# Attention pairs: a pair's factors and division one unit of scores later, and the latent key copies ahead of the last query tile's rotation

## What is computed

```python
s = jnp.einsum('bqkgd,btkd->bkgqt', qblk, k).astype(jnp.float32) * scale
p = jax.nn.softmax(s, axis=-1).astype(v.dtype)
return jnp.einsum('bkgqt,btkd->bqkgd', p, v)
...
merged = jnp.concatenate([rms_norm(o_g, out_norm_gqa), rms_norm(o_m, out_norm_mla)], axis=-1)
return merged @ w_o
```

## Time and profile before

| what | us |
|---|---|
| runs of the kernel, median (lowest to highest) | 2344.77 (2344.0 to 2347.44) |
| the profiled execution | 2343.82 |
| its span | 2341.9 |
| TensorE busy, share of the span | 2279.8 (97%) |
| TensorE's weight loads | 1636.5 (70%) |
| VectorE | 1332.9 (57%) |
| ScalarE | 879.0 (38%) |
| GpSimd | 230.0 (10%) |

### The profile page before, as it was taken

How to read it: one execution, slowest core, us unless ns; L and a number is a source line. 1 busy time by engine, 2 the same in 40 slices (tenths; PEclk the granted TensorE clock), 3 DMA queues, 4 the chain that set the end, 5 groups by cost and what they waited for, 6 DMA issues and landing times.

```text
span 2341.9 us, 28359 instructions
## 1 busy us (share of the span) xinstructions
PE 2279.8 (97%) x10908; PEld 1636.5 (70%) x10908; DVE 1332.9 (57%) x2055; ACT 879.0 (38%) x1518; POOL 230.0 (10%) x190
## 2 busy tenths in 40 slices
PE   7999999999998999999999999999999999999998
PEld 6755876444675588644457788888888778888886
DVE  5676654323657665433347757777435665877722
ACT  4475542111437644211133234444223233444421
POOL 2212201000220220100000011000001002000000
PEclk9999999999999999999999999999999999999999
DMA  4300439999530024899974333333333323333331
GB/s 174 99 5 24 141 149 386 409 410 410 210 99 15 19 90 180 339 408 410 410 299 122 86 90 90 99 98 92 99 98 136 112 77 91 99 99 98 101 97 48
DMA packets 112085, 381.62 MB, mean 163 GB/s; under 512 B 16464, under 2 KB 17232, under 8 KB 111696
## 3 DMA queue, kind: packets, MB, share of 16 engines
q1 hardware_dynamic: 108208, 366.80, 44.8%
q0 software_dynamic: 2304, 8.39, 0.9%
q10 hardware_dynamic: 1440, 4.62, 0.5%
HBM read 363.51 MB, written 6.29 MB: 158 GB/s over the span
## 4 chain that ended last, share of the span: by engine, by line
PE 87%; DVE 6%; ACT 3%; DMA 2%; POOL 1%; issue 1%; SPq 0%; POOLq 0%; DVEq 0%; ACTq 0%
PE ps L1349 11%; PE ps L1350 11%; PE ps L1351 11%; PE ps L1654 9%; PE ps L1373 5%; PE ps L1374 5%; PE ps L1375 5%; PE ps L1676 5%; PE ps L1535 3%; PE ps L1394 3%; PE ps L1392 3%; PE ps L1393 3%; PE ps L1485 2%; PE ps L1493 2%; PE ps L1686 1%; PE ps L1687 1%
## 5 line engine op out<-in xcount | busy, mean ns | idle before, releaser
L2464 DVE TENSOR_TENSOR wlo<-stage,whi 128x1024 fp32r<-128x1024 f32 x262 | 329.2, 1260 | 279.2 <-ACT whi L1793 278.6
L1349 PE MATMUL ps<-hTh,whi 128*128 128x512 f32 x1120 | 443.2, 396 | 0.0
L1351 PE MATMUL ps<-hTh,wlo 128*128 128x512 f32 x1120 | 438.0, 391 | 0.0
L1350 PE MATMUL ps<-hTl,whi 128*128 128x512 f32 x1120 | 437.7, 391 | 0.0
L1793 ACT ACTIVATE whi<-stage 128x1024 fp32r<-128x1024 f32 x262 | 276.0, 1057 | 328.4 <-PE ps L1375 120.7
L1349 PEld LDWEIGHTS ps<-hTh,whi 128*128 128x128 f32 x1120 | 211.6, 189 | 48.6 <-issue 4.7
L1351 PEld LDWEIGHTS ps<-hTh,wlo 128*128 128x128 f32 x1120 | 211.2, 189 | 44.7
L1350 PEld LDWEIGHTS ps<-hTl,whi 128*128 128x128 f32 x1120 | 211.6, 189 | 42.7
L2379 DVE TENSOR_TENSOR ps<-ps,Rs 128x512 f32<-128x512 f32 x124 | 86.0, 698 | 140.3 <-PE ps L1351 126.2
L2382 DVE SCALAR_TENSOR_TENSOR t<-ps,vecs,t 128x511 f32<-128x511 f32 (+1 forms) x176 | 131.0, 744 | 3.8 <-ACT t L1756 0.7
L2379 DVE TENSOR_TENSOR x<-x,ps 128x512 f32<-128x512 f32 x184 | 116.4, 680 | 28.5 <-PE ps L1375 18.0
(11 more groups left out here) (382 smaller groups left out, 4209.4 us busy)
## 6 DMA issues: line engine op xcount, KB each, us to landing
stage<-in_wpk SPq DMA_DIRECT2D x268, 512.0 KB, 3.6
wa<-in_wd SPq DMA_DIRECT2D x56, 512.0 KB, 15.5
wa<-in_wu SPq DMA_DIRECT2D x54, 512.0 KB, 15.1
wa<-in_wg SPq DMA_DIRECT2D x46, 512.0 KB, 14.3
ws<-in_wg SPq DMA_DIRECT2D x26, 512.0 KB, 12.4
ws<-in_wu SPq DMA_DIRECT2D x24, 512.0 KB, 11.1
wr<-in_wg SPq DMA_DIRECT2D x24, 512.0 KB, 15.2
stage<-in_wd SPq DMA_DIRECT2D x22, 512.0 KB, 16.4
```

The source lines that it names most:

```text
L1349: pe.matmul(o, h, ah, start=k == 0, stop=False)
L1350: pe.matmul(o, h, al, start=False, stop=False)
L1351: t = pe.matmul(o, lo, ah, start=False, stop=k == 7)
L2464: ve.tensor_tensor(M.wlo[i % NW][:, :], M.stage[i % NSTAGE][:, :], f(M.whi[i % NW][:, :]), ALU.subtract).then_inc(*S.wlo.mark(("w", i)))
```

## The change

It has two parts. First, the step `att_out` of the mixer is split. `att_copy` (ScalarE's copy of the values to `oT`) stays behind the values; the turn of the factors (`shares`), VectorE's product and all that `att_sums` puts off move into the next tick, which runs behind the next unit's scores. For the last pair (`p == 7`) they stay where they were. Second, the rotation of q3 is put off by two more ticks, so that in VectorE's program it comes behind the four copies of the latent keys.

```diff
@@ attention(), values()
             if kt == KT - 1:
-                b = self.take()
-                self.do("shares", l, p, b)
-                self.do("att_out", kind, l, p, ub[p], b)
+                self.do("att_copy", l, p, ub[p])
                 self.drop(ub[p])
-                self.drop(b)
-                self.att_sums(l, p)
+
+                def divide():
+                    b = self.take()
+                    self.do("shares", l, p, b)
+                    self.do("att_out", kind, l, p, b)
+                    self.drop(b)
+                    self.att_sums(l, p)
+                if p == 7:
+                    divide()
+                else:
+                    self.later.append(divide)
@@ mixer(), head_tile()
-                    self.later.append((lambda: self.last.append(st3)) if tile == "q3" else st3)
+                    if tile == "q3":
+                        self.last.append(lambda: self.last.append(lambda: self.last.append(st3)))
+                    else:
+                        self.later.append(st3)
@@ ScalarE's program
+        elif name == "att_copy":
+            l, p, u = a
+            q.wait_ge(*S.pe.at("values", "mix", l, p))
+            if p in (4, 0):
+                q.wait_ge(*S.dve.at("heads", l, "k"))
+                q.wait_ge(*S.dve.at("heads", l, "q0"))
+            copy(M.oT[:, POS["mix"][p], :], M.ps[u[0]][:, :], ("oU", l, p), ("free",) + u)
```

More of the change, by code:

```diff
@@ L1920, in act_program @@
                  ("PT", "mem", l, d), ("free",) + u)
+        elif name == "att_copy":
[5 more added lines that the diff above has]
+            copy(M.oT[:, POS["mix"][p], :], M.ps[u[0]][:, :], ("oU", l, p), ("free",) + u)
         elif name == "att_out":
-            kind, l, p, u, *_ = a
+            kind, l, p, u = a
             if kind == "mem":
@@ L1927, in act_program @@
                 continue
[L1928 to L1932, removed]
             if p == 7:
@@ L2645, in dve_program @@
         elif name == "att_out":
-            kind, l, p, u, *b = a
+            kind, l, p, u = a
             if kind == "mix":
@@ L2650, in dve_program @@
                 o = M.oT[:, POS["mix"][p], :]
-                tt(o, o, M.ps[b[0][0]][:, :], ALU.mult, ("oT", l, p), ("free",) + b[0])
+                tt(o, o, M.ps[u[0]][:, :], ALU.mult, ("oT", l, p), ("free",) + u)
             if kind == "mem":
```

## The result

The changed kernel took 2332.06 us (median of 4 runs, 2330.8 to 2332.44), the kernel before 2346.11 us beside it (4 runs, 2344.0 to 2347.62). The ratio is 0.9944, 95% interval 0.9932 to 0.9956, so it is faster by 0.56%. Run again with the last experiments the two took 2331.14 and 2342.99 us, ratio 0.9949, interval 0.9936 to 0.9963. The profiled execution after took 2332.44 us against 2343.82 before: 11.4 us less, where 11.2 were forecast.

The account below looks back on a forecast made before the run. TensorE, busy for 97% of the span, was taken as the bound. Seven terms sum to 5.6 us a layer, 11.2 for both: 2343.82 - 11.2 = 2332.6 profiled, median 0.95 higher, 2333.6, range 2329 to 2340.

Parts of the forecast that it names:

- Start: Start of attention: key copies fill VectorE's idle time before q3's swap, so first maximum and scores come earlier; 1.94 us a layer.
- First and second boundary: First two value boundaries: VectorE has no gap, so little is gained despite 2.42 us idle noted; 0.05 us each.
- Third boundary: Third value boundary: query remainder no longer overlaps GpSimd's squares, taking 0.7 for 1.80, and TensorE's 1.34 wait goes; 1.15 us.
- Fourth boundary: Fourth value boundary: no remainder there, so the earlier maximum is passed on and TensorE recovers what it idled; 0.6 us.
- Fifth boundary to the sixth: Sixth pair's values: group outputs come later, so the stop shortens, a new wait of 0.8 paid in it; 1.3 us.
- End: End of attention: sum of squares moves behind the last scores, which start 0.85 earlier; gain 0.5 us.
- Passed on whole: Behind attention: memory stage and experts' loads are gated by TensorE's steps, so the whole 11.2 us reaches the end.
- Saturated engines: Rival: VectorE has the same work, boundaries give nothing, only start and end gain 4.9 us; 2339.9 us, chance 0.13.
- The gain swallowed behind attention: Rival: time won is lost behind attention to the experts' weight stream; 2344.8 us, chance 0.06.
- Banks: Rival: the factors' bank is held longer, TensorE waits 1.06 us at the turn at 14 boundaries; 2355.7 us, chance 0.04.
- The clock's fall: Rival: lower granted clock at 637 to 644 us, one fall more or less, some 3 us; within 0.05 left for unseen things.
- The overlap with GpSimd: Third boundary: VectorE's two-SBUF-input remainder is fully blocked by GpSimd, 1.80 for 0.69; full block would end some 0.1 later than seen.

Follow-up runs that it names:

- the last experiments: Kernel with second group output later, plus query remainders later, last half chunk later, or both; and the changed kernel unaltered: 2329.48, 2330.71, 2330.55, 2331.14 us.
- the division alone: Kernel before with only the first part of the change, factors and division one unit later, rotation of q3 unmoved: 2337.05 us, ratio 0.9965.
- The rotation alone: Kernel before with only the second part of the change, q3's rotation put behind the key copies: 2339.05 us, ratio 0.9984.
- the square waits: Kernel before with one wait more: GpSimd's square of the third pair waits until VectorE's last query remainder is made: 2340.30 us, ratio 0.9984.
- the sums later: Kernel before with only the sums of squares and what follows them one unit later, values, factors and products unmoved: 2340.17 us, ratio 0.9987.

## Why the prediction was right

The time was forecast at 2333.6 within 2329 to 2340 and came out at 2332.06; the profiled execution at 2332.6, and came out at 2332.44. Some of this closeness is luck. In attention the first layer won 0.1 us less than the 5.6 of the sum and the second 0.2 more, the latter by 0.35 at the third boundary that no term of the sum held; and the kernel before, beside it, took 1.3 us more than the 2344.77 from which the forecast was made, so that the difference of the medians, 14.05, is further from 11.2 than the times are from each other. Step by step:

**Start, 1.94 forecast, 1.74 measured.** Right in mechanism, mis-sized by 0.2. The rows after:

```profile
101.99 1.91 DVE L2394 SCALAR_TENSOR_TENSOR mq<-ps,mcs 64x512 f32<-64x512 f32 x3
103.93 2.52 DVE L2609 COPY mk<-ps 64x512 f32<-64x512 f32 x4
...
104.51 2.64 ACT L1766 ACTIVATE vm<-ps 128x512 f32<-128x512 f32 x4
...
106.35 2.73 PE L1495 MATMUL ps<-mk,mq 128*128 128x512 f32 x6
...
106.48 0.69 DVE L2391 TENSOR_TENSOR sq<-sq,sing 128x512 f32<-128x512 f32 x1
107.28 0.69 DVE L2391 TENSOR_TENSOR raw<-tmp,sq 128x512 f32<-128x512 f32 x1
108.00 1.29 DVE L2617 TENSOR_REDUCE st<-ps 128x1 f32<-128x512 f32 x2
```

The key copies stand right behind the latent queries, without idle time, as said. The first scores start at 106.35 with no wait noted, 0.8 us before ScalarE's `vm` copies end (104.51 + 2.64 = 107.15), so they do not wait for the end of these, and the reading that they had waited for VectorE's first key copy stands. The missing 0.2 is in "the rotation takes 106.99 - 105.59 = 1.40": now it is 108.00 - 106.48 = 1.52, since the maximum behind it starts 0.72 after the rotation's last instruction, where the copy had started 0.60 after it; the rest is a few hundredths at each hand-over.

**First and second boundary, 0.05 each.** Right: 0.04 and 0.05 for the two together, although had named 22.2 us of waiting and the earlier trace rows 2.42 us of it there.

**Third boundary, 1.15.** Right in the first layer to the hundredth; the second layer gave 1.50. The remainder took 0.69, and one wait of 0.62 is left where there had been one of 0.24 (at 158.05) and one of 1.34:

```profile
154.88 0.69 DVE L2394 SCALAR_TENSOR_TENSOR qs<-raw,qs 64x512 fp32r<-64x512 f32 x1
...
156.37 1.04 POOL L2195 TENSOR_TENSOR raw<-oT 128x512 f32<-128x512 f32 x1 [11.80 <-DVE oT L2391]
...
157.76 0.66 PE L1503 MATMUL ps<-c,Pr 128*128 128x128 f32 x4 [0.62 <-ACT Pr L1766]
```

The experiment that only holds GpSimd back gave 1.11 and 1.10 here, so the overlap was the cause. It doesn't give the second layer's further 0.35, which the division alone does give. That is a wait of another kind, which I missed by working out one layer and doubling it. In the kernel before, at this boundary of the second layer alone, VectorE's product starts 1.02 behind ScalarE's copy in place of 0.66, and the wait is put down to TensorE's next turn:

```profile
748.97 0.60 ACT L1756 ACTIVATE oT<-ps 128x512 f32<-128x512 f32 x1 [0.30 <-PE ps L1535]
...
749.99 0.69 DVE L2379 TENSOR_TENSOR oT<-oT,ps 128x512 f32<-128x512 f32 x1 [2.78 <-PE ps L1493]
```

What stands behind the product is late with it, and TensorE waits 0.59 at 752.83 where it waited 0.24 in the first layer. The rotation alone, the square waits and the sums later, which leave the product where it was, all have it (1.01, 1.01 and 1.00); with the product behind the remainder, in the division alone and in the changed kernel, no product of this boundary has a wait noted. Why it waits for that turn in the second layer only stays open.

**Fourth boundary, 0.6.** Right: 0.67 and 0.68.

**Fifth boundary to the sixth, 1.3.** The amount is right, 1.25 and 1.15, and so are its parts: a new wait of 0.57 (0.8 was the forecast), and a stop of the values of 191.73 to 193.09 in place of 195.10 to 197.73.

```profile
187.26 0.65 PE L1432 MATMUL ps<-c,st 128*128 128x128 f32 x4 [0.57 <-POOL st L2147]
...
190.24 1.56 POOL L2219 TENSOR_TENSOR ygl<-tmp,ygh 128x512 fp32r<-128x512 f32 x1 [3.04 <-ACT ygh L1766]
...
190.59 1.76 DVE L2394 SCALAR_TENSOR_TENSOR tmp<-oT,vecs,raw 128x512 f32<-128x512 f32 x1
...
192.27 0.68 DVE L2633 COPY PT<-ps 128x512 f32<-128x512 f32 x1
...
193.09 3.62 PE L1545 MATMUL ps<-PT,vm 128*64 128x512 f32 x14 [0.29 <-ACT ygh L1766]
```

One reason given was incomplete: "everything of the group comes one unit later". The sums-later kernel has exactly that and keeps 0.46 of the 1.25; the product has to be behind the maximum as well, or the late `oT` holds VectorE up. I had not looked at who stands behind the product there. And the new wait, counted as paid in the 1.3, is worth nothing by itself: taken away, it came back as 0.57 more of the stop.

**End, 0.5.** Right, mis-sized by 0.15: 0.64 and 0.65. The wait of 0.72 is gone.

```profile
218.16 1.14 PE L1503 MATMUL ps<-c,tmp 128*128 128x128 f32 x8
```

**Passed on whole.** Right: attention is 11.26 us shorter and the span 11.4; from the last copy of the second layer to the end of the span it is 1517.8 us before and 1517.9 after.

**The rivals.** Saturated engines (2339.9) fell: the boundaries gave 6.5 us of the 11.26. The gain swallowed behind attention fell with the span. Banks: no turn of a boundary has a new wait for `PT` or for a bank; the 1.06 of the earlier trace rows is as it was. The clock's fall ahead of the second layer is still there and as deep: over the 7 us that lie as far ahead of the last `mq` as 637 to 644 us did before (59.19 us), the mean is 0.53 where it was 0.56; the stretch between the two attentions (eighth copy to last `mq`) took 466.49 us after 466.89, so it decided nothing.

**The overlap with GpSimd.** Here the trace said that the remainder, begun just behind GpSimd's sum, ended 0.55 after it, and the runs agree: 155.20 + 1.28 to 155.84 + 1.19 is 0.55, 201.22 + 1.27 to 201.68 + 1.36 is 0.55, 190.24 + 1.56 to 190.59 + 1.76 is 0.55. The Trainium skill (SBUF — State Buffer, section Who interferes with whom) has the instruction that comes second fully blocked until the other is done. The runs agree with it, save that it then ends some 0.14 us sooner than its own 0.69 (the output, which takes 0.75 alone, 0.20 sooner); that was the open 0.1 of the prediction.

## What to carry to other kernels

A long wait in the view of who waits for whom may be one engine starving while another is busy; the gain of removing it is found only by following, at each place, what the waiting engine does first when work comes back, and what the critical engine next needs of it. Reading that way gave seven terms, of which none was off by more than 0.2 us in the layer from which they were worked out.

A wait on the critical engine is not a cost until it is known that the next wait would not take its place: removing the 0.57 us at the factor's turn won nothing, removing a 1.3 us stop won 0.8. And when a producer is moved, move its consumers as far; the division moved without its sums would have lost 4.1 of the 5.5 us.

Where the steps are smaller than the spread of whole runs, compare a stretch inside the trace, from one marker to another; here it repeats to 0.1 us, while whole runs of one kernel differ by up to 8.

## What the runs showed of the hardware

**The recorded starts do not tell who is blocked.** In the trace of the changed kernel the same three instructions come out differently in the two layers. In the first, GpSimd's subtraction is recorded from 190.24 and VectorE's copy that spreads the reciprocals (`tmp<-st`) from 190.25; yet it is the subtraction that was held: it took 1.56 in place of 1.27, the copy its 0.43, and the output that began 0.35 behind the subtraction 1.76. The second layer, VectorE and then GpSimd:

```profile
778.74 1.55 DVE L2654 COPY tmp<-st 128x512 f32<-128x512 f32 x1
...
780.22 0.74 DVE L2394 SCALAR_TENSOR_TENSOR tmp<-oT,vecs,raw 128x512 f32<-128x512 f32 x1
```

```profile
778.74 1.27 POOL L2219 TENSOR_TENSOR ygl<-tmp,ygh 128x512 fp32r<-128x512 f32 x1 [3.03 <-ACT ygh L1766]
```

Both start at 778.74, and now the subtraction is undisturbed, the copy takes 1.55 and the output after it 0.74. The sum is nearly the same (from the copy's start to the output's end 2.10 and 2.22 us), so the layers differ by 0.1 us in the end (32.50 and 32.60 us between the fifth and the seventh copy). Traced again, the same kernel had both layers as the first is here (1.56, 0.43, 1.76), and 32.50 and 32.49 us. This copy from SBUF to SBUF was thus blocked like an operation of two SBUF inputs. In each case the blocked one ends sooner behind the other than it takes alone, by 0.14 to 0.20 us: VectorE's remainder 0.55 for 0.69, its output 0.55 for 0.75, its copy 0.28 for 0.43, GpSimd's subtraction 1.12 for 1.27.

**The spread lies outside attention.** Two traces of one and the same program, the changed kernel, in the stretch of 43 to 50 us; the first is the one above with a granted clock of 0.62, this is the other:

```profile
43.00:50.00 7.00, 5.65 (x27) 4.65 (x27) 5.09 (x9) 2.77 (x4) 1.03 (x2) 0.77 0.21 69
```

A mean of 0.62 or 0.77 means that the lower of the two levels (1.2 GHz, 0.5) was granted for about 5.3 or 3.2 of the 7 us, estimated from the two means. The last `mq` of the first layer started at 101.99 in the one and 101.29 in the other, and between 100.70 and 103.47 over the traces of all kernels, which are the same up to there but for the place of q3's rotation; the stretch between the two attentions, from the eighth copy to the last `mq`, took 465.1 to 467.8 us. What sets how long the lower level lasts was not tested.
